# Norms between stages: block 0 by halves of 256 tokens, products with the rounded input one block ahead, squares added in wide pairs

## The reference, cut to what matters

```
def rms_norm(x, g):
    xf = x.astype(jnp.float32)
    y = xf * lax.rsqrt(jnp.mean(xf * xf, axis=-1, keepdims=True) + RMS_EPS)
    return (y * g.astype(jnp.float32)).astype(x.dtype)
...
        h = h + rms_norm(y, mix_norm_post[layer])
        f = swiglu(rms_norm(h, ffn_norm_pre[layer]), ffn_w_gate_up[layer], ffn_w_down[layer])
        h = h + rms_norm(f, ffn_norm_post[layer])
```

## Time and profile before

| | us |
|---|---|
| three runs | 2150.64, 2152.36, 2152.63 (median 2152.36) |
| the profiled execution | 2152.26 |
| its span, first to last instruction | 2150.5 |
| TensorE multiplying (PE busy) | 2087.3, 97% of the span |
| VectorE, ACT busy | 1169.1, 704.5 |
| mean granted TensorE clock | 0.989 of full speed |

### The profile page before, as it was taken

One profiled execution on the slowest core, in us unless ns is written; L12 is line 12 of the kernel. 1 busy time (PEld: TensorE's weight loads), 2 busy tenths in 40 slices (PEclk: granted clock), 3 DMA queues, 4 the chain that ended last, 5 costly groups with the idle time before them and its releaser, 6 DMA issues.

```text
span 2150.5 us, 25943 instructions
## 1 busy us (share of the span) xinstructions
PE 2087.3 (97%) x10181; PEld 1718.8 (80%) x10181; DVE 1169.1 (54%) x1959; ACT 704.5 (33%) x1038; POOL 9.7 (0%) x23
## 2 busy tenths in 40 slices
PE   7999999999999999999998999999998899999997
PEld 5887888888788898888976788888787678888885
DVE  5656544432775756757657644432489756444323
ACT  4324322221523323333234422221334553222211
POOL 0000000000000000000000000000000000000000
PEclk9999999999999999999999999999999999999998
DMA  4772222232124151251411222232222121222321
GB/s 170 113 107 85 98 97 98 88 107 98 62 96 137 60 137 60 72 144 60 126 52 59 79 91 100 86 114 95 102 79 79 40 98 66 98 91 98 107 94 52
DMA packets 35913, 198.53 MB, mean 92 GB/s; under 512 B 3911, under 2 KB 4456, under 8 KB 14456
## 3 DMA queue, kind: packets, MB, share of 16 engines
q1 hardware_dynamic: 28248, 182.13, 24.3%
q10 hardware_dynamic: 6656, 12.58, 2.7%
q0 software_dynamic: 928, 2.70, 2.6%
HBM read 181.14 MB, written 3.67 MB: 86 GB/s over the span
## 4 chain that ended last, share of the span: by engine, by line
PE 91%; DVE 6%; ACT 2%; issue 1%; DMA 0%; SPq 0%; DVEq 0%; ACTq 0%
PE bank L1425 82%; PE bank L1650 3%; PE bank L1612 2%; PE bank L1461 1%; PE bank L1628 1%; DVE c L1296 1%; DVE work L885 1%; ACT w_hi L496 1%; DVE p L1136 0%; DVE w_lo L837 0%; DVE w_lo L839 0%; PE bank L1526 0%; PE bank L1667 0%; DVE v1s L1107 0%; PE bank L1528 0%
## 5 line engine op out<-in xcount | busy, mean ns | idle before, releaser
L1425 PE MATMUL bank<-x_hi,w_hi 128*128 128x512 f32 x1760 | 700.1, 398 | 16.0 <-DVE x_lo L849 12.4
L1425 PE MATMUL bank<-x_hi,w_lo 128*128 128x512 f32 x1760 | 687.3, 391 | 0.0
L1425 PE MATMUL bank<-x_lo,w_hi 128*128 128x512 f32 x1760 | 686.5, 390 | 0.0
L837 DVE TENSOR_TENSOR w_lo<-w_raw,w_hi 128x2048 fp32r<-128x2048 f32 x131 | 299.9, 2291 | 439.2 <-ACT w_hi L496 439.2
L1425 PEld LDWEIGHTS bank<-x_hi,w_hi 128*128 128x128 f32 x1760 | 331.3, 188 | 95.4 <-issue 24.9
L1425 PEld LDWEIGHTS bank<-x_hi,w_lo 128*128 128x128 f32 x1760 | 331.0, 188 | 70.4
L1425 PEld LDWEIGHTS bank<-x_lo,w_hi 128*128 128x128 f32 x1760 | 331.5, 188 | 67.4 <-issue 1.4
L496 ACT ACTIVATE w_hi<-w_raw 128x2048 fp32r<-128x2048 f32 x131 | 249.6, 1908 | 339.1 <-PE bank L1425 322.5
L1425 PE MATMUL bank<-ff_hi,w_hi 128*128 (+1 forms) x528 | 205.4, 389 | 0.0
L1425 PE MATMUL bank<-ff_lo,w_hi 128*128 (+1 forms) x528 | 205.4, 389 | 0.0
L1425 PE MATMUL bank<-ff_hi,w_lo 128*128 (+1 forms) x528 | 205.4, 389 | 0.0
(11 more groups left out here) (192 smaller groups left out, 2032.5 us busy)
## 6 DMA issues: line engine op xcount, KB each, us to landing
w_raw<-w_all SPq DMA_DIRECT2D x167, 1024.0 KB, 4.9
qk<-qk_next ACTq DMA_DIRECT2D x32, 384.0 KB, 10.6
w_raw<-w_all SPq DMA_DIRECT2D x8, 256.0 KB, 6.2
h<-x_t SPq DMA_DIRECT2D x4, 512.0 KB, 7.0
out_t<-h SPq DMA_DIRECT2D x8, 256.0 KB, 2.0
skew<-erow POOLq DMA_DIRECT2D x8, 192.0 KB, 8.7
bias<-skew POOLq DMA_DIRECT2D x8, 128.0 KB, 2.3
pos_i<-pos SPq DMA_DIRECT2D x1, 256.0 KB
```

The source lines that it names most:

```text
L837: ins = v.tensor_tensor(w_lo[p][:, part], raw, hi, ALU.subtract)
L1425: ins = mm(out, b if flip else a, a if flip else b, start=start and n == 0, stop=stop and n == 2, **kw)
```

## The change

WARM goes from 30 to 13. In seams 1 to 5 the post-norm's statistic is summed and its factor made in two halves of 256 tokens (first half in bank 0, second in bank 5), and block 0 goes through multiply, add and rounded copy by the same halves. TensorE starts with the products of x_hi and both weight parts for the first half of block 0, then the second half; from block 1 on it issues the 8 products with x_hi[k], then the 4 with x_lo[k-1]. x_lo of block m - 1 is made after the add of block m. The squares go to an array of their own (sq, eight blocks), are added two blocks at a time (128x1024) and folded by one 128x512 add at the end. Both first units end together, then the statistic follows; TensorE waits for r_pre before the fourth unit. ACT rounds last + 4 before that factor, VectorE splits last + 3 and last + 4 at the end of the seam, and the first pair (or l == 1) does not any more. Behind seam 2 the 8 one-column products go from before the third unit to before the seventh. The start of the kernel (t = 0) and the last seam (t = 6) stay as they were, but for counts.

```diff
-WARM = 30
+WARM = 13
...
+HALVES = [slice(0, S // 2), slice(S // 2, S)]
...
+        sq = sb("sq", [P, KC, S], at=region + K16)
...
         @block.scalar
...
-                act.wait_ge(ystat_done, t)
-                rstd(bank[0][:], work[:, RQ, :], D, yr_ready)
+                for hf in range(2 if t < 6 else 1):
+                    act.wait_ge(ystat_done, 2 * t - 1 + hf)
+                    c = HALVES[hf] if t < 6 else slice(0, S)
+                    rstd(bank[5 * hf][:, c], work[:, RQ, c], D, yr_ready)
...
             def pre_norm_rstd(t):
                 if t == 0:
                     round_unit(2)
+                else:
+                    round_unit(LAST_ROWS[t] + 4)
                 act.wait_ge(xstat_done, t + 1)
                 rstd(bank[3][:], r_pre[:], D, xr_ready)
 
             def pre_norm(t):
 
-                for m in range(KC):
-                    act.wait_ge(h_ready, KC * (t - 1) + m + 1)
-                    pre_norm_block(t, m)
+                for hf in range(2):
+                    act.wait_ge(h_ready, blocks_ready(t, 0) - 1 + hf)
+                    pre_norm_hi(t, 0, HALVES[hf])
+                pre_norm_square(t, 0)
+                for m in range(1, KC):
+                    act.wait_ge(h_ready, blocks_ready(t, m))
+                    pre_norm_hi(t, m)
+                    pre_norm_square(t, m)
                 pre_norm_rstd(t)
...
-                    round_unit(u0 + l + 3, i, 4)
+                    if not first:
+                        round_unit(u0 + l + 3, i, 4)
...
         @block.vector
...
+            def xadd_pair(t, n):
+
+                dve.wait_ge(xsq_done, KC * t + 2 * n + 2)
+                if n > 1:
+                    dve.wait_ge(xacc_done, 7 + 4 * (t - 1) + n - 1)
+                v.tensor_tensor(sq[:, 0:2, :], sq[:, 0:2, :], sq[:, 2 * n:2 * n + 2, :], ALU.add).then_inc(xacc_done, 1)
+
+            def xadd_last(t):
+
+                dve.wait_ge(xacc_done, 7 + 4 * (t - 1) + 3)
+                v.tensor_tensor(sq[:, 0, :], sq[:, 0, :], sq[:, 1, :], ALU.add).then_inc(xacc_done, 1)
...
             def transition(t):
                 post_norm(t)
+                for hf in range(2):
+                    dve.wait_ge(yr_ready, 2 * t - 1 + hf)
+                    residual(t, 0, HALVES[hf])
+                for m in range(1, KC):
+                    residual(t, m)
+                    xlo(t, m - 1)
+                    if m in (4, 6):
+                        xadd_pair(t, m // 2 - 1)
+                xlo(t, KC - 1)
+                xadd_pair(t, 3)
+                xadd_last(t)
+                for n in (3, 4):
+                    rest_unit(LAST_ROWS[t] + n)
...
-                    rest_unit(u0 + l + 3, i, 4)
+                    if not first:
+                        rest_unit(u0 + l + 3, i, 4)
...
-            dve.wait_ge(rcol_ps, 1)
-            v.tensor_copy(r_col[:], bank[2][:, 0:8]).then_inc(rcol_ready, 1)
+            order.wait()
             v.memset(cm, 0.0).then_inc(at_out, 1)
-            dve.wait_ge(rcol_ready, 1)
...
                 elif lam == 6:
+                    v.tensor_copy(r_col[:], bank[2][:, 0:8]).then_inc(rcol_ready, 1)
+                    dve.wait_ge(rcol_ready, 1)
...
         @block.tensor
...
+            def seam_products(u, k, part, x, c=slice(0, S)):
+
+                for l in range(2):
+                    for m in range(2):
+                        ins = mm(banks_of(l)[m][:, c], weights(u + l, k * 256 + m * P)[part], x[:, k, c],
+                                 start=k == 0 and part == 0 and x is x_hi and c.start == 0,
+                                 stop=k == KC - 1 and x is x_lo, skip_group_check=True)
+                    if k == KC - 1 and x is x_lo:
+                        ins.then_inc(unit_done, 1)
+
+            def seam_units(t, u):
+
+                for _ in range(WARM):
+                    mm(bank[4][:, 0:3 * P], ident_b[:], mask_b[:], start=True, stop=True)
+                pe.wait_ge(w_split, u + 2)
+                for hf in range(2):
+                    pe.wait_ge(xhi_done, rounded_count(t, 0) - 1 + hf)
+                    for part in range(2):
+                        seam_products(u, 0, part, x_hi, HALVES[hf])
+                for k in range(1, KC):
+                    pe.wait_ge(xhi_done, rounded_count(t, k))
+                    for part in range(2):
+                        seam_products(u, k, part, x_hi)
+                    pe.wait_ge(x_ready, KC * t + k)
+                    seam_products(u, k - 1, 0, x_lo)
+                pe.wait_ge(x_ready, KC * (t + 1))
+                seam_products(u, KC - 1, 0, x_lo)
+                xstat(t)
...
+                for hf in range(2):
+                    mm(bank[5 * hf][:, HALVES[hf]], ones[:], work[:, 0, HALVES[hf]], start=True, stop=False)
                 pe.wait_ge(ysq_done, KC * t)
-                mm(bank[0][:], ones[:], work[:, 2, :], start=False, stop=True).then_inc(ystat_done, 1)
+                for hf in range(2):
+                    mm(bank[5 * hf][:, HALVES[hf]], ones[:], work[:, 2, HALVES[hf]], start=False,
+                       stop=True).then_inc(ystat_done, 1)
...
                 if lam == 3:
-                    pe.wait_ge(rcol_ready, 1)
+                    pe.wait_ge(xr_ready, 3)
                 unit(QKV + lam, lam, EV_QKV)
             pe.wait_ge(evac, EV_QKV + 4)
+            for n in range(8):
+                cols = slice(n, S, 4) if n < 4 else slice((n - 4) * P, (n - 3) * P)
+                ins = mm(bank[2][:, n:n + 1], r_pre[0:1, cols], ones[0:1, 0:1], start=True, stop=True)
+            ins.then_inc(rcol_ps, 1)
             v0_unit(QKV + 6)
```

More of the change, by code:

```diff
@@ L888, in post_norm, with residual, transition_end @@
                     rest_unit(last + 2)
[L889 to L894, removed]
-                                                  work[:, RQ, :], ALU.mult, ALU.mult))
-                if t < 6 and m == 1:
-                    xlo(t, 0)
+                if t == 6:
+                    dve.wait_ge(yr_ready, 2 * 5 + 1)
+            def residual(t, m, c=slice(0, S)):
+                src = bank[m][:, c] if m in KEPT[t] else y[:, m, c]
+                order.mark(v.scalar_tensor_tensor(work[:, TMP + m % 2, c], src, gain(POST_GAIN[t] + m),
+                                                  work[:, RQ, c], ALU.mult, ALU.mult))
                 order.wait()
-                v.tensor_tensor(h[:, m, :], h[:, m, :], work[:, TMP + m % 2, :], ALU.add).then_inc(h_ready, 1)
+                v.tensor_tensor(h[:, m, c], h[:, m, c], work[:, TMP + m % 2, c], ALU.add).then_inc(h_ready, 1)
             def transition(t):
                 post_norm(t)
-                for m in range(KC):
-                    residual(t, m)
-                    if t < 6 and m >= 2:
-                        xlo(t, m - 1)
-                        xadd(t, m - 2)
-                if t < 6:
-                    xlo(t, KC - 1)
-                    xadd(t, KC - 2)
-                    xadd(t, KC - 1)
-                    rest_unit(LAST_ROWS[t] + 3)
+                for hf in range(2):
[11 more added lines that the diff above has]
+                    rest_unit(LAST_ROWS[t] + n)
+            def transition_end():
+                post_norm(6)
+                for m in range(KC):
+                    residual(6, m)
             def scaled(dst, src, r=None):
@@ L1412, in _ @@
             down(DOWN_C)
-            transition(6)
+            transition_end()
         @block.tensor
@@ L1451, in xstat, with first_units @@
             def xstat(t):
[L1452 to L1455 removed]
+                pe.wait_ge(xacc_done, 7 + 4 * t)
+                mm(bank[3][:], ones[:], sq[:, 0, :] if t else work[:, 0, :], start=True, stop=True).then_inc(xstat_done, 1)
+            def seam_products(u, k, part, x, c=slice(0, S)):
[23 more added lines that the diff above has]
+                xstat(t)
+            def first_units(u):
                 early = 5
[L1458 to L1462 removed]
                 def first_piece(k):
@@ L1562, in _ @@
             down(2, DOWN_A, EV_QKV, 0)
-            first_units(2, QKV)
-            for n in range(8):
-                cols = slice(n, S, 4) if n < 4 else slice((n - 4) * P, (n - 3) * P)
-                ins = mm(bank[2][:, n:n + 1], r_pre[0:1, cols], ones[0:1, 0:1], start=True, stop=True)
-            ins.then_inc(rcol_ps, 1)
+            seam_units(2, QKV)
             def v0_unit(u):
```

82 lines of the change are left out of this document (45 added, 37 removed).

## The result

| | before | after |
|---|---|---|
| median of the runs, us | 2152.45 (4 runs, 2150.64 to 2152.63) | 2139.78 (4 runs, 2137.92 to 2141.88) |
| profiled execution, us | 2152.26 | 2141.36 |
| its span, us | 2150.5 | 2139.6 |
| mean granted clock in it | 0.989 | 0.989 |

The ratio is 0.9941 [0.9929, 0.9952]: 0.6% faster, with the whole interval under 1; 12.7 us in the medians and 10.9 in the profiled pair, where the forecast said 9.3. The median lies 0.02 us under the low end of the range, the profiled execution inside it.

What follows compares the result with a forecast made beforehand. TensorE, once started, was taken as the bound; only its start is late. Gains of 5.2 (seams 1, 4, 5), 1.7 (seam 2) and 2.4 us (seam 3) sum to 9.3: 2152.3 - 9.3 = 2143.0 us, range 2139.8 to 2148.5.

Steps and rivals of the forecast that it cites:

- A = S + 0.54: Seam 1: the first half's factor is ready 0.54 us after the old end of the post-norm's statistic.
- the first rival: Weight loads, busy 0.188 us each, set the half products' step: gain only 6.0 us, 2146.3 us; chance 0.06.
- 128x1024 add, 1.22 on the line through both: Wide add of squares, not in the trace: 1.22 us, read between 0.69 and 2.29 us; no gain by itself.
- the third: Rival: wide adds cost as the 2048 row, 1.07 us more each, holding the third unit: 2149.5 us; chance 0.04.
- the signs: Listed trace marks of a right forecast, among them a 0.4 to 0.5 us stall before block 1, none behind.
- The second rival: The halves bring nothing: some 0.5 to 0.9 us a seam, 4 in all, 2148 us; chance 0.06.
- 88 products run through, at this seam's pace of 0.230 us: Seams 1, 4, 5: from block 1 on, TensorE's products run without a stall and take 20.24 us.
- From there it is never idle: Seam 1 before the change: TensorE has no idle time from the warm-up's end at 200.80 us.
- TensorE starts 0.15 us behind its operand: Products with the rounded input: start 0.15 us after the operand; the first product takes 0.13 us above the pace.
- partly covered: Seam 2's one-column passes, 2.92 us, partly hidden before the seventh unit: 2.4 us taken in the low end.
- this costs nothing with a margin of 2 us: Seam end: VectorE's sums and moved weight splits finish before TensorE wants them, 2 us to spare.
- seam 2's term of 4.6 us: Fourth unit behind seam 2 at 601.6 against 606.19 us; net 1.7 us after the one-column passes' 2.92.

## Why the prediction was right or wrong, point by point

**Right: what bounds it, and that the gain passes.** TensorE's pieces behind the seams kept their length, and each seam's gain stood at the end. *A = S + 0.54* was 0.53; *first half A + 1.67* was A + 1.66; half products 0.12 apart, so loads of 188 ns do not set the step, and the first rival falls. *128x1024 add, 1.22 on the line through both* was 1.22, and with it the third. A stall stood before block 1 (0.38 us by the starts in seam 1, near the 0.4 to 0.5 of the signs, none at seam 3) and none behind. No third unit waited for a split. The second rival falls with the run without halves.

**Wrong: the step "88 products run through, at this seam's pace of 0.230 us".** I had the pace by dividing a whole stretch of before by its 95 products, and that stretch held a stall: two steps of 0.35 and 0.33 at block 6, where TensorE waited for VectorE. "From there it is never idle" overlooked this wait. After, where x_lo comes a block late in the order, the wait is gone and the 88 products take 0.2268 each (220.12 - 200.04, less 0.12 for the first, over 88): 0.28 us less than 20.24. I had the right number beside it: 0.2275 and 0.2273 for seams 2 and 3, which have no stall, and there the misses are 0.2 and 0.1. That the forecast used another pace for three seams of five was the hint. The wide adds alone (S + 27.49) confirm that it was a wait. The low end of the range did allow for this pace (0.8 us), so this step made the sum too small but did not take the result out of the range.

**The same step, smaller: "TensorE starts 0.15 us behind its operand".** True of the first product (197.53 to 197.67), but block 1's operand was there at 199.98 and its product started at 200.04: 0.06. With a copy ready 0.02 earlier, block 1 came at A + 4.03 instead of 4.14. 0.28 + 0.11 + 0.01 = 0.40 is seam 1's miss (2.16 against 1.76). Seams 1, 4 and 5 gave 6.4 us where 5.2 were counted, seams 2 and 3 0.3 more than forecast: that is the 1.5 us between 9.3 and 10.8.

**Wrong: the range had no term for the level of the runs.** This is what took the result out, by 0.02 us. The seams' 10.8 us would have given 2141.5, well inside; the rest up to 12.7 us is the four runs' median, halfway between two levels 3.5 us apart. Ten more runs put it at 10.7 and 11.2 under before, inside the range, so that these four fell just outside is chance. The range's low end came from terms of the sum alone, and the larger of them, 2.4 us for one-column passes partly covered, did not come true. That the levels go with the granted clock is shown; why an execution takes one or the other is not.

**Right, but for less than the whole reason: "this costs nothing with a margin of 2 us".** The moved splits held up no third unit. But I treated the move as a cost to be covered, and it is the reason why 9 of the 11 us arrive, half of them as waits and the rest mainly by the clock behind them: seam 2's *fourth unit follows 48 products later* only because its split no longer stands behind the rotations (waits of 2.87 and 1.82 us when put back). I had used that fact in seam 2's term of 4.6 us (measured 4.95, by the fourth unit's second product, 606.49 - 562.53 against 598.96 - 559.95) and in one sentence on the stage behind seam 4, without a price for it.

**Right: the one-column passes**, 2.85 us in the chain; "partly covered", which I allowed in the low end, did not come about, and spread among products they cost more.

**Warm-up, "no term of its own".** Right at 13; but 30 take the whole gain and 0 lose 4 us, so it is a condition of every other term. The parts undone one at a time (order 11, halves 4, weights 9, 30 warm-up products 13 us) sum to far more than 11: each of these holds TensorE up again, by a wait or by idle products that run too long, and with the old order and the old place of the weights' work the clock fell behind the wait too.

## What to carry to other kernels

Read a pace from neighbouring starts in a piece without a wait; a mean over a stretch hides stalls that the change may remove, and two seams with different means are the sign of one. When a critical engine starts sooner, its next inputs (here the splits of the weights) must come sooner too: price what happens if they do not, for that price is the worth of moving them. Here the best of three numbers of idle products ahead of late real work was the one that ended just when the first operand came: too many displace it, and with none the clock fell at two of the four seams where 13 had held it. A filling that keeps the clock at one place is proved by the kernel's time, not by that place: here half clock showed up at other rests.

## What the runs showed of the hardware that was not expected

Rests of one length met two answers of the clock. Without warm-up products TensorE rested 2.19 us in front of the first half in seams 1, 4 and 5, and only at seam 4 did half speed follow; and with the old order a rest of 2.44 us in seam 1 brought half speed, one of 2.85 us in seam 2 none. One kernel can also differ from itself: when the changed kernel ran again, its profile showed the seventh unit at half clock behind the one-column passes, which the result's profile does not (the stretch in that execution, then in the result's):

```profile
634.00:642.00 8.00, 8.00 (x39) 7.99 (x40) 5.92 (x9) 1.55 (x3) 0.00 (x0) 0.57 0.12 23
```

```profile
634.00:642.00 8.00, 8.00 (x68) 7.99 (x68) 4.63 (x7) 0.20 (x1) 0.00 (x0) 1.00 0.28 90
```

39 and 68 products in the same 8 us. At 0.57 the mean holds some 6.9 us of half clock, 3.4 us of work, about the distance between the two levels of the runs; that the levels are made of such places is likely, not shown. And a fp32 pass of one column costs far more than its column: 2.85 us for 16, 0.18 each, where a rounded product of 256 columns takes 0.12; spread among such products a pair costs more still.
